# Expert weights fetched as 1 MB transfers over two buffers, gate weights in whole rows, one expert loop on TensorE

## What is computed

```python
for e in range(N_EXPERTS):            # 16 experts
    hid = jax.nn.silu(t @ w_expert_gate[e]) * (t @ w_expert_up[e])     # 1024 -> 512
    y = y + combine[:, e:e + 1] * (hid @ w_expert_down[e])             # 512 -> 1024
```

## Time and profile before

| | us |
|---|---|
| median of 3 runs (889.49 to 890.2) | 889.65 |
| the profiled execution, its own time | 890.09 |
| its span, first to last instruction | 888.3 |
| TensorE busy (94% of the span) | 834.4 |
| VectorE busy | 603.9 |
| ScalarE busy | 518.5 |
| expert items, from the first matmul to the last | about 568 to 868 |

### The profile page before, as it was taken

How to read it: one execution, slowest core, us unless ns; L and a number is a source line. 1 busy time by engine, 2 the same in 40 slices (tenths; PEclk the granted TensorE clock), 3 DMA queues, 4 the chain that set the end, 5 groups by cost and what they waited for, 6 DMA issues and landing times.

```text
span 888.3 us, 15492 instructions
## 1 busy us (share of the span) xinstructions
PE 834.4 (94%) x4963; PEld 737.7 (83%) x4963; DVE 603.9 (68%) x1026; ACT 518.5 (58%) x965; POOL 83.7 (9%) x73
## 2 busy tenths in 40 slices
PE   4999999999999999999999998999999999999891
PEld 3999999899989898989997887878777787778670
DVE  6363233687778778466555137689999898998684
ACT  7243214566656666455623232488888788878584
POOL 0000000000000000000000001122233222321020
PEclk9999999999999999999999999999999999999896
DMA  8622222133123212331236746599999999999974
GB/s 260 153 75 80 75 69 72 57 103 85 45 73 102 84 49 78 120 95 49 96 95 210 230 175 228 175 308 337 323 344 342 344 340 338 339 333 335 339 258 156
DMA packets 154392, 163.77 MB, mean 184 GB/s; under 512 B 20596, under 2 KB 138484, under 8 KB 154346
## 3 DMA queue, kind: packets, MB, share of 16 engines
q1 hardware_dynamic: 148538, 151.12, 52.1%
q0 software_dynamic: 5520, 11.45, 4.7%
q10 hardware_dynamic: 288, 0.59, 0.2%
HBM read 151.61 MB, written 20.12 MB: 193 GB/s over the span
## 4 chain that ended last, share of the span: by engine, by line
PE 48%; DVE 5%; DMA 2%; SPq 2%; issue 2%; ACT 1%; POOLq 0%; POOL 0%; DVEq 0%; ACTq 0%
PE ps L1542 14%; PE ps L1544 13%; PE ps L1543 13%; SPq L493 2%; DMA rawM<-in_w_expert_up 1%; PE ps L1906 1%; PE ps L1828 1%; PE ps L1926 1%; PE ps L1835 1%; DVE ob L1513 1%; DMA xg<-h_rows,idi 0%; PE ps L1820 0%; PE ps L1859 0%; DVE wl L1458 0%; PE ps L1860 0%
## 5 line engine op out<-in xcount | busy, mean ns | idle before, releaser
L1458 DVE TENSOR_TENSOR wl<-rawM,wh 128x1024 fp32r<-128x1024 f32 x189 | 223.6, 1220 | 25.3 <-ACT wh L913 23.5
L913 ACT ACTIVATE wh<-rawM 128x1024 fp32r<-128x1024 f32 x192 | 196.0, 1054 | 10.8 <-PE ps L1544 9.0
L1542 PE MATMUL ps<-hTh,wh 128*128 128x272 f32 x448 | 132.2, 295 | 1.6 <-ACT qkv L773 0.9
L1544 PE MATMUL ps<-hTh,wl 128*128 128x272 f32 x448 | 130.4, 291 | 0.0
L1543 PE MATMUL ps<-hTl,wh 128*128 128x272 f32 x448 | 129.7, 289 | 0.0
L1542 PE MATMUL ps<-wh,xh 128*128 128x512 f32 x256 | 105.3, 412 | 4.3 <-issue 4.3
L1543 PE MATMUL ps<-wl,xh 128*128 128x512 f32 x256 | 102.2, 399 | 0.0
L1544 PE MATMUL ps<-wh,xl 128*128 128x512 f32 x256 | 102.2, 399 | 0.0
L1542 PE MATMUL ps<-wh,hTh 128*128 128x384 f32 x256 | 94.5, 369 | 5.1 <-ACT qkv L773 3.6
L1542 PEld LDWEIGHTS ps<-hTh,wh 128*128 128x128 f32 x448 | 85.3, 190 | 3.3 <-ACT qkv L773 1.3
L1544 PE MATMUL ps<-wh,hTl 128*128 128x384 f32 x256 | 86.5, 338 | 0.0
(11 more groups left out here) (300 smaller groups left out, 1682.0 us busy)
## 6 DMA issues: line engine op xcount, KB each, us to landing
rawM<-in_w_expert_gate SPq DMA_DIRECT2D x128, 256.0 KB, 5.2
rawM<-in_w_expert_up SPq DMA_DIRECT2D x128, 256.0 KB, 7.4
rawM<-in_w_expert_down SPq DMA_DIRECT2D x64, 512.0 KB, 8.2
rawA<-in_w_in SPq DMA_DIRECT2D x64, 192.0 KB, 3.0
rawA<-in_w_in SPq DMA_DIRECT2D x20, 512.0 KB, 5.5
rawA<-in_w_attn_branch SPq DMA_DIRECT2D x8, 512.0 KB, 4.1
rawA<-in_w_out SPq DMA_DIRECT2D x8, 512.0 KB, 4.2
x<-in_x_prompt SPq DMA_DIRECT2D x4, 512.0 KB, 6.8
```

The source lines that it names most:

```text
L913: nc.scalar.activation(wh[:, (c + 1) % S, :], rawM[:, slot, :], ACT.Copy).then_inc(m_hi, 1)
L1458: V.tensor_tensor(wl[:, sl, :], rawM[:, slot, :], wh[:, sl, :].bitcast(F32), ALU.subtract).then_inc(m_lo, 1)
L1542: T.matmul(out, sh, mh_, start=start, stop=False, **kw)
L1544: return T.matmul(out, sl, mh_, start=False, stop=stop, **kw)
```

## The change

- **Transfers.** `moe_load` now fills two slots with one transfer of 1 MB. Gate weights fill chunks 0 to 3 and are read in whole rows of 512 columns (2 KB); up weights fill chunks 4 and 5 (columns 0 to 255) and 6 and 7 (columns 256 to 511) in 1 KB rows; down weights keep 4 KB rows. An item has 6 transfers, not 20. `next_load` waits until both slots are free, and the split waits for the whole 1 MB.
- **Matmuls.** A gate chunk is still 6 matmuls of 512 columns (into bank 0). An up chunk is 12 matmuls of 256 columns (banks 1 and 7). An item has 108 matmuls with their weight loads, not 84.
- **Hidden values.** Gate is complete after chunk 3 and gets one silu of 512 columns. The first half of `hid` now needs chunk 5 and is transposed after chunk 6; the second needs chunk 7.
- **Loop.** TensorE has items 0 to 13 in one loop; `xg_lo` counts in twos, so that item 0 needs no code of its own.
- **Start.** The transfers before the loop are cut at other slots (10 to 21 early, then 0 to 3, 4 to 9, 22 and 23).

```diff
             def moe_load(slot, e, c):
-                d = rawM[:, slot, :]
-                if c < 8:
-                    half, q = divmod(c, 4)
-                    d = d.rearrange("p (k m n) -> p k m n", k=2, m=2)
-                    for m in range(2):
-                        src = moe_src[m][e, 2 * P * q:2 * P * (q + 1), 256 * half:256 * (half + 1)]
-                        sp.dma_start(d[:, :, m, :], src.rearrange("(k p) n -> p k n", p=P)).then_inc(m_raw[slot], 16)
+                d = rawM[:, slot:slot + 2, :]
+                if c < 4:
+                    sp.dma_start(d.rearrange("p s (k n) -> p (s k) n", k=2), moe_src[0][e, 2 * P * c:2 * P * (c + 2), :].rearrange(
+                        "(k p) n -> p k n", p=P)).then_inc(m_raw[slot], 16)
+                elif c < 8:
+                    half = (c - 4) // 2
+                    sp.dma_start(d.rearrange("p s (k n) -> p (s k) n", k=4),
+                                 moe_src[1][e, :, 256 * half:256 * (half + 1)].rearrange(
+                                     "(k p) n -> p k n", p=P)).then_inc(m_raw[slot], 16)
...
-                sp.wait_ge(m_lo, n - RM + 1)
+                sp.wait_ge(m_lo, n - RM + 2)
...
-                act.wait_ge(m_raw[slot], (32 if c < 8 else 16) * (rnd + 1))
+                act.wait_ge(m_raw[slot - c % 2], 16 * (rnd + 1))
...
+                act.wait_ge(m_mm, n0 + 5)
+                act.wait_ge(hid_done, 2 * i + 1)
+                nc.scalar.activation(hsl[:], ps[:, 0, :], ACT.Silu).then_inc(si_done, 1)
                 for half in range(2):
-                    act.wait_ge(m_mm, n0 + 4 * half + 5)
-                    act.wait_ge(hid_done, 2 * i + half + 1)
-                    nc.scalar.activation(hsl[:, 256 * half:256 * half + 256], ps[:, half, 0:256], ACT.Silu).then_inc(si_done, 1)
-                    for c in ((7, 8) if half == 0 else (10,)):
+                    for c in ((7, 8, 9) if half == 0 else (10, 11)):
                         ahead(c)
...
+                def hidden(half):
+                    hs = slice(256 * half, 256 * half + 256)
+                    if half == 0:
+                        dve.wait_ge(si_done, i + 1)
+                    dve.wait_ge(m_mm, n0 + 2 * half + 7)
+                    V.tensor_tensor(hid[:, hs], ps[:, UP_BANKS[half], 0:256], hsl[:, hs], ALU.mult).then_inc(hid_done, 1)
...
+                ahead(7)
+                ahead(8)
+                hidden(0)
+                ahead(9)
+                hidden_lo(0)
+                hidden(1)
+                ahead(10)
+                ahead(11)
+                hidden_lo(1)
+                ahead(12)
...
-                    for kk in range(2):
-                        k = 2 * (c % 4) + kk
-                        wc = slice(512 * kk, 512 * kk + 512)
-                        ins = three(ps[:, c // 4, :], xh[:, k, :], xl[:, k, :], wh[:, (c + 1) % S, wc], wl[:, (c + 1) % S, wc],
-                                    k == 0, k == KD - 1)
+                    rows, width = (2, 512) if c < 4 else (4, 256)
+                    bank = 0 if c < 4 else UP_BANKS[(c - 4) // 2]
+                    for kk in range(rows):
+                        k = rows * (c % 4 if c < 4 else c % 2) + kk
+                        wc = slice(width * kk, width * kk + width)
+                        ins = three(ps[:, bank, 0:width], xh[:, k, :], xl[:, k, :], wh[:, (c + 1) % S, wc],
+                                    wl[:, (c + 1) % S, wc], k == 0, k == KD - 1)
...
-                for c in range(6):
+                for c in range(7):
...
                 turn_hidden(0)
-                up(6)
                 up(7)
...
-            item(0, 0, first=True)
-            item(0, 1)
-            with pe.Fori(1, EXPERTS // 2 - 1) as ip:
+            with pe.Fori(0, EXPERTS // 2 - 1) as ip:
```

More of the change, by code:

```diff
@@ L499, in _ @@
             sp.wait_ge(ab_lo, 5)
-            early = [4] + list(range(9, RM - 2))
-            for s in early:
+            early = list(range(10, RM - 2))
+            for s in early[::2]:
                 moe_load(s, s // 12, s % 12)
             sp.wait_ge(o_mm, NT)
-            for s in range(4):
+            for s in range(0, 4, 2):
                 moe_load(s, s // 12, s % 12)
@@ L515, in _ @@
             sp.wait_ge(o_mm, 2 * NT)
-            for s in range(4, 9):
-                if s not in early:
-                    moe_load(s, s // 12, s % 12)
+            for s in range(4, 10, 2):
+                moe_load(s, s // 12, s % 12)
             start_sums(NT - 1)
@@ L535, in _ @@
                 for par in range(2):
-                    for c in range(12):
+                    for c in range(0, 12, 2):
                         next_load(12 * par + c, 2 * ip + 2 + par, c, 24 * ip + 24 + 12 * par + c)
@@ L1461, in item, with hidden_lo @@
                     ahead(c)
-                for half in range(2):
+                def hidden(half):
[4 more added lines that the diff above has]
+                    V.tensor_tensor(hid[:, hs], ps[:, UP_BANKS[half], 0:256], hsl[:, hs], ALU.mult).then_inc(hid_done, 1)
+                def hidden_lo(half):
                     hs = slice(256 * half, 256 * half + 256)
                     kk = slice(2 * half, 2 * half + 2)
-                    dve.wait_ge(si_done, 2 * i + half + 1)
-                    V.tensor_tensor(hid[:, hs], ps[:, half, 256:512], hsl[:, hs], ALU.mult).then_inc(hid_done, 1)
-                    for c in ((7, 8) if half == 0 else (10,)):
-                        ahead(c)
                     dve.wait_ge(hid_hi, 2 * i + half + 1)
@@ L1471, in item @@
                                     hh[:, kk, :].bitcast(F32), ALU.subtract).then_inc(hid_lo, 1)
-                    for c in ((9,) if half == 0 else (11, 12)):
-                        ahead(c)
+                ahead(7)
[7 more added lines that the diff above has]
+                hidden_lo(1)
+                ahead(12)
                 if final:
@@ L1484, in rows @@
                                 ps[:, 2:4, :].rearrange("p b (k n) -> p b k n", k=4),
[L1485 removed]
+                                xh[:].bitcast(F32).rearrange("p (b k) n -> p b k n", b=2), ALU.subtract).then_inc(xg_lo, 2)
             m_lo_split(2)
@@ L1907, in gathered, with item @@
                 ins.then_inc(xg_mm, 1)
-            def item(ip, par, final=False, first=False):
+            def item(ip, par, final=False):
                 i = 2 * ip + par
```

19 lines of the change are left out of this document (8 added, 11 removed).

## The result

The changed kernel takes 893.4 us (median of 13 runs) beside 889.79 for the kernel before in the same comparison: ratio 1.0039, 95% interval 1.0028 to 1.0051, slower by 3.6 us. One of the 13 executions of the kernel before took 1361.7 us, and the ratio leaves such slow runs out. The prediction had the sign right and twice the size, +7.2 us. The profiled execution took 893.4 us itself, with a span of 891.1 us (before: 890.09 and 888.3).

A forecast was written before the change was run, and what follows sets the result against it. TensorE's instructions were taken to bound the kernel, not the full DMA queue. Sixteen items at +0.51 us less 1.0 at the end, exit unchanged, gave +7.2 us: 896.8 us, likeliest case 892.5 to 900.7, stated range 889.0 to 900.5.

The forecast's parts named there:

- The matmuls: TensorE, per item: 48 matmuls of 256 columns at 0.118 us replace 24 of 512, +0.06 us, up to +0.40.
- The item, +0.51 us: Each item on TensorE grows from 18.34 to 18.85 us, mainly by waiting for the first half of `hid`.
- The chain that was worked out: From chunk 4's start S: silu, copy, two subtracts, `hid`; transposes can start at S + 4.70, TensorE waits 0.45 us.
- An item therefore takes what its instructions take: Expert stage before the change: TensorE is busy throughout, so its instructions alone set the item's 18.34 us.
- The exit, 0: TensorE's loop exit: the jump remains, and so do its costs of 4.4 us gap and 2.5 us lower clock.
- The late transfer disappears; it was hidden under the fetch.: Loop exit: 8.9 us of new queue reserve ends item 14's late transfer, alone worth 0.7 us, with no gain.
- What remains of the gap: Loop exit: most of TensorE's gap is the fetch of the code behind the jump; 4 to 5 us stay.
- The rival of a loop that no longer fits: TensorE's longer loop must fetch instructions at each return, adding 26 to 41 us: 923 to 938 us; chance 0.06.
- The end, -1.0: Last item: chunk 11's copy moves ahead of the last transposes on ScalarE, so about 1.0 us comes back.
- The queue: Weight transfers go from 20.5 to about 20.1 us an expert, worth nothing while TensorE does not wait for them.
- the prediction's three signs of being wrong: No TensorE wait ahead of the transposes, item 14 starting without a gap, or a gap at each loop return.
- The rival of the late transfer: Loop exit: the late transfer caused the gap, so new reserve returns 6.9 us: 889.9 us, no change; chance 0.08.

The follow-up runs named there:

- Experiment 2: Changed kernel with the first half of `hid` one subtract later on VectorE, behind chunk 9 too: 910.03 us, ratio 1.023.
- 5: Changed kernel with `hid` and `hl` each one subtract earlier on VectorE, 1 MB transfers kept: 887.18 us, ratio 0.9974.
- 6: Changed kernel with `hid` and `hl` each one subtract earlier and 512 KB transfers, gate rows still 2 KB: 884.31 us, ratio 0.9935.
- experiment 17: Kernel before with a loop of 60 unused semaphore increments on TensorE ahead of the items: 920.87 us, increments included.
- experiment 4: Kernel before with only TensorE's loop changed, items 0 to 13 in one loop: 889.4 us, ratio 1.0001.
- 7: Kernel before without TensorE's loop over further tiles, so no jump at the exit: 887.33 us, ratio 0.9973.
- 8: Kernel before with one TensorE loop whose end is computed, nothing left out: 887.36 us, ratio 0.9982.
- 9: Changed kernel with `hid` and `hl` moved up, 512 KB transfers and one TensorE loop with a computed end: 883.82 us, ratio 0.9928.
- 13: Changed kernel with one TensorE loop whose end is computed: 888.33 us, ratio 0.9982.
- 16: Kernel before with 128 unused semaphore increments in a row on TensorE ahead of the loop: 907.0 us, increments included.
- 18: Kernel before with 64 unused semaphore increments in a row on TensorE ahead of the items: 897.41 us, increments included.
- experiment 10: Changed kernel with its own VectorE order and 512 KB transfers, gate rows still whole: 893.7 us, ratio 1.0043.
- 1: Changed kernel with the first half of `hid` one subtract earlier on VectorE, ahead of chunk 8's: 893.48 us, ratio 1.0049.
- 3: Kernel before with only the transfers changed, 1 MB over two buffers, gate rows still 1 KB: 892.02 us, ratio 1.0031.

## Why the prediction was half right

**The matmuls.** 0.1177 us for 256 columns, 0.118 taken. Right.

**The item, +0.51 us: a term was missing.** Measured +0.37. The chain that was worked out came nearly as forecast. It reached the transposes at S + 4.62, not 4.70 (silu's follower at S + 0.79 and handovers a little shorter), so they wait 0.38 us, not 0.45; but they and chunk 7 then take 0.08 us more than in before. From chunk 4 to `down(0)` before needs 653.05 - 647.23 = 5.82 us, the changed kernel 654.73 - 648.42 = 6.31: +0.49. What the sum had at nothing is the turn to the next item. "An item therefore takes what its instructions take" is not quite so: in before VectorE comes to `xl` straight from two subtracts, `xl` is ready at 659.74, 0.23 us behind the start of the last `down` matmul at 659.51, and 0.35 us pass to the next item's first matmul, in place of 0.23. In the changed kernel VectorE has time to spare there (it waits 0.82 us for `xh`), `xl` is ready with that matmul, and 0.23 us pass (642.50 to 642.73). The new order so gives 0.12 us back at each item's start. Experiment 2 shows that `hid`'s place sets the item, experiments 5 and 6 that without it the changed matmuls and rows take 18.10 to 18.25 us. Over 16 items the term is 5.7 us in place of 8.2.

**The exit, 0: the step that failed.** "The late transfer disappears; it was hidden under the fetch." It did disappear, but it had not been hidden, and the exit came out 1.94 us shorter. Some 0.85 us of this are the gap (0.98 less the 0.12 that before loses at every turn), 1.1 the clock: item 14 takes 2.6 us more than the others in before (829.24 to 850.17 us, at first at 1.2 GHz) and 1.54 in the changed kernel (833.20 to 853.44). The first instruction of the next item waits for `xl`, and in both kernels the fetch starts 0.5 to 0.9 us behind `xl` or the last matmul, whichever is later. I had read the 3.7 us between `xl` and TensorE's start as proof that the tokens did not matter; a serial chain looks just so. No run changed the tokens' time alone (experiment 17 was to, and did not), and experiments 4 to 6 start their fetch otherwise; so the serial wait is supported by these rows, not isolated.

The clock's part is not explained by the gap's length: gaps of 4.7 us had eleven to thirteen slow matmuls, but 4.5 and 4.9 us (6 and 17) seven or eight, like the gaps of 3.7. So this 1.1 us came in two profiles of two, but the change is not shown to be what gave it back.

**What remains of the gap** is the fetch, as the prediction said: without a jump it is gone (7, 8, 9, 13), though another place of the code took it away too (16, 18). The Trainium skill, page "Runtime: NRT & Kernel Launch", section "Instruction fetch mechanics", says that a taken branch outside the window waits for a DMA fetch of the target's block; the exits agree (2.7 to 3.1 us from the transfer's start to the next matmul), and so does the 0.02 MB of each. By its two-block window of 512 instructions the changed loop, of which the trace has 471 TensorE instructions in a turn, is near fetching at its returns; by the 2048 that the same section gives TensorE it is far from it. No `q8` transfer falls between 600 and 829 us and no return has a gap, which fits both. The rival of a loop that no longer fits is false for this loop.

**The end, -1.0.** -0.94: the table load follows the last transposes by 0.82 us where it was 1.76. Right.

**The queue.** 20.1 us an expert, as forecast, and no wait for `rawM`. That the megabyte's coarse wait costs nothing here was right too, for the reason given (experiment 10); with faster items it costs 2.9 us (5 against 6).

**The sum.** 5.7 - 0.94 - 1.94 = +2.8 us, the difference of the profiled spans; the medians differ by 3.6 (interval 2.5 to 4.5). Forecast was 8.2 - 1.0 + 0 = +7.2. The item's 2.5 us (1.9 of them the missing 0.12 an item) and the exit's 1.9 err to the same side, and together they are the miss. None of the prediction's three signs of being wrong appeared: the wait, a gap (if shorter than forecast) and the quiet returns are all there. The rival of the late transfer (chance 0.08) was false as put, since most of the gap stayed, but it named what the main case left out.

## What to carry to other kernels

When stages swap their order, walk the chain through every engine's queue with measured durations, and then walk the next one: moving one product out of a wait moved the wait to its successor (1), and only moving both gave 6 us, and 9 with small transfers (5, 6). When a wait and a fetch or a transfer meet at one gap, don't let the longer hide the shorter until the trace shows that they start independently: look whether the fetch begins before or after the wait ends. And a gap on the busiest engine may be what lets the queue and the row transfers catch up, so its removal pays in full only where they have reserve: 5.1 us in the changed kernel, 2.1 in before, 0.5 in the fastest. So follow the chain that ended last anew after each gain: in 8 and 9 it had moved to other work.

## What the runs showed that I had not expected

- Whether TensorE waits for code at a loop's exit can depend on where the code lies: 64 or 128 instructions more ahead of the loop of before took a gap of 4.7 us to 1.4 and 0.7; 96 and 192 in the changed kernel changed nothing. The jump passes over one more loop body, some 377 TensorE instructions in before and 471 in the changed kernel; it is the shorter jump whose stall came and went. What the boundary is stays open.
- An increment of a semaphore on TensorE, in a row of them, took some 0.15 us: 96 made item 0 longer by 32.87 - 18.05 = 14.8 us, a few matmuls at 1.2 GHz included.
- The length of a gap does not tell what the clock does. After 3.0 us (experiment 4) it stayed at 2.4 GHz, but after 2.75 us (3) eight matmuls of 512 columns ran at 1.2 GHz; after 4.7 us twelve, after 4.9 us (17) some seven.
- A loop whose end is a register's value cost nothing measurable over a constant one (13).
- The fastest kernel (9), the changed one with `hid` and `hl` moved up, 512 KB transfers and the computed end, took 883.82 us, 5.9 below the kernel before and 9.6 below the changed one.
